# Sparse attention: the compressed branch's scores formed inside the unit loop, one key-value group at a time

## What is computed

```python
s = jnp.einsum('bgmqd,bgnd->bgmqn', qb, kc)                  # kc: 31 compressed keys per group
p_cmp = masked_softmax(s, cmp_end[None, :] <= tq[:, None])
p_cmp = p_cmp * (tq >= CMP_BLOCK - 1).astype(jnp.float32)[:, None]
o_cmp = jnp.einsum('bgmqn,bgnd->bgmqd', p_cmp.astype(vc.dtype), vc)
...
o = jnp.stack([o_cmp, o_sel, o_win], axis=-1).reshape(b, NSA_HEADS, Q_BLOCK, d, 3)
return jnp.einsum('bhqdc,bhqc->bqhd', o, gb)                 # gated sum of the three
```

## Time and profile before

| | |
|---|---|
| median of 3 runs | 1906.64 us (1906.56 to 1907.07) |
| the profiled execution | 1915.09 us, its span 1912.6 us |
| PE busy | 1802.2 us, 94% of the span |
| DVE, ACT, POOL busy | 748.1, 562.1, 201.2 us |
| attention's units (L1424 to L1457) | 733.9 to 834 us in the span |

### The profile page before, as it was taken

The page is one execution under the profiler, slowest core; times in us unless marked ns, Lnnn a source line. Parts: engine busy times, 40 slices in busy tenths (PEclk is TensorE's granted clock), DMA queues, the critical chain, the costliest instruction groups (busy, mean ns, idle before and its releaser), DMA issues. The chain is left out here.

```text
span 1912.6 us, 21769 instructions
## 1 busy us (share of the span) xinstructions
PE 1802.2 (94%) x9065; PEld 1337.2 (70%) x9065; DVE 748.1 (39%) x1121; ACT 562.1 (29%) x871; POOL 201.2 (11%) x229
## 2 busy tenths in 40 slices
PE   7998999999999999998999999989999987999993
PEld 6777888888878786567888888878777773333331
DVE  4425322233265345735222232362345553222334
ACT  4325222232252124635222222352346410000001
POOL 3000000000001103310000000000001102323322
PEclk9979999999999998999999999999999987999997
DMA  7212333322323117312333323233220056999983
GB/s 225 95 39 66 95 103 88 108 90 90 109 95 109 66 58 221 99 34 61 105 88 107 91 89 110 89 121 94 72 111 23 17 206 271 371 381 396 381 325 145
DMA packets 178451, 260.21 MB, mean 136 GB/s; under 512 B 18873, under 2 KB 134777, under 8 KB 165953
## 3 DMA queue, kind: packets, MB, share of 16 engines
q1 hardware_dynamic: 154768, 202.56, 31.6%
q0 software_dynamic: 19568, 27.13, 4.5%
q10 hardware_dynamic: 4032, 29.36, 3.9%
HBM read 296.78 MB, written 29.40 MB: 171 GB/s over the span
## 5 line engine op out<-in xcount | busy, mean ns | idle before, releaser
L149 DVE TENSOR_TENSOR RING_R<-RING,RING_R 128x2048 fp32r<-128x2048 f32 (+1 forms) x110 | 250.2, 2277 | 664.9 <-ACT RING_R L146 664.9
L168 PE MATMUL PB<-RING_R,OPS_R 128*128 128x512 f32 (+1 forms) x1056 | 415.1, 393 | 11.1 <-DVE RING_R L149 5.2
L169 PE MATMUL PB<-RING_R,OPS_R 128*128 128x512 f32 (+1 forms) x1056 | 410.0, 388 | 0.0
L170 PE MATMUL PB<-RING_R,OPS_R 128*128 128x512 f32 (+1 forms) x1056 | 409.9, 388 | 0.0
L146 ACT ACTIVATE RING_R<-RING 128x2048 fp32r<-128x2048 f32 (+1 forms) x110 | 208.4, 1897 | 333.5 <-DMA RING<-in_ffn_w_down 138.1
L168 PE MATMUL PB<-OPS_R,RING_R 128*128 128x512 f32 (+1 forms) x736 | 282.5, 384 | 7.9 <-DVE OPS_R L275 7.9
L169 PE MATMUL PB<-OPS_R,RING_R 128*128 128x512 f32 (+1 forms) x736 | 281.8, 383 | 0.0
L170 PE MATMUL PB<-OPS_R,RING_R 128*128 128x512 f32 (+1 forms) x736 | 281.7, 383 | 0.0
L168 PEld LDWEIGHTS PB<-RING_R,OPS_R 128*128 128x128 f32 x1056 | 199.6, 189 | 54.9 <-DVE RING_R L149 6.9
L170 PEld LDWEIGHTS PB<-RING_R,OPS_R 128*128 128x128 f32 x1056 | 199.5, 189 | 41.0
L169 PEld LDWEIGHTS PB<-RING_R,OPS_R 128*128 128x128 f32 x1056 | 199.9, 189 | 39.1
(11 more groups left out here) (361 smaller groups left out, 1883.9 us busy)
## 6 DMA issues: line engine op xcount, KB each, us to landing
RING<-in_ffn_w_gate SPq DMA_DIRECT2D x44, 512.0 KB, 4.0
RING<-in_ffn_w_up SPq DMA_DIRECT2D x44, 512.0 KB, 5.2
RING<-in_ffn_w_down SPq DMA_DIRECT2D x44, 512.0 KB, 3.9
RING<-in_w_expert_gate SPq DMA_DIRECT2D x16, 1024.0 KB, 8.1
RING<-in_w_expert_up SPq DMA_DIRECT2D x16, 1024.0 KB, 11.6
OPS<-in_w_expert_gate SPq DMA_DIRECT2D x16, 1024.0 KB, 11.3
OPS<-in_w_expert_up SPq DMA_DIRECT2D x16, 1024.0 KB, 13.4
Y<-in_w_expert_down ACTq DMA_DIRECT2D x14, 1024.0 KB, 9.5
```

The source lines that it names most:

```text
L149: nc.vector.tensor_tensor(RING_R[:, raw], RING[:, raw], RING_R[:, high].bitcast(fp32), ALU.subtract).then_inc(s_wlo, 1)
L168: nc.tensor.matmul(o, x[0], w[0], start=start, stop=False)
L169: nc.tensor.matmul(o, x[0], w[1], start=False, stop=False)
L170: return nc.tensor.matmul(o, x[1], w[0], start=False, stop=stop)
```

## The change

The compressed scores are no longer formed ahead of the loop. `cmp_scores(a)` forms those of one group in bank 7: group 0 in step 0, group 1 in step 1, each after `scores(u + 2)` and `values(u - 1)` and ahead of `turned(u)`. The second waits until DVE has taken the first out of bank 7. PE's wait ahead of the loop goes. DVE takes each group by itself (`cmp_max`, 128x512) at the end of steps 0 and 1. Exponential, sum and POOL's scaling come one step later (2; 3; 3 and 4), and the values of `a_cr` are renumbered.

```diff
@@ nsa_pe @@
+            def cmp_scores(a):
+                if a:
+                    pe.wait_ge(a_cr, 2)
+                h = slice(a * DH, (a + 1) * DH)
+                nc.tensor.matmul(PB[:, 7, :], ident_b[:], cmask_b[:].unsqueeze(2).to_broadcast([P, MT, 4, NQ]),
+                                 start=True, stop=False)
+                for i in range(MT):
+                    for c in range(4):
+                        t = nc.tensor.matmul(PB[:, 7, (4 * i + c) * NQ:(4 * i + c + 1) * NQ], qTn[h, c, i * P:(i + 1) * P],
+                                             kcT[h, :], start=False, stop=(i == MT - 1 and c == 3))
+                t.then_inc(a_cs, 1)
+
             def turn_cmp(a):
-                pe.wait_ge(a_cr, 6 + a)
+                pe.wait_ge(a_cr, 8 + a)
@@ nsa_pe, ahead of the loop and in it @@
-            for a in range(2):
-                nc.tensor.matmul(PB[:, 4 + a, :], ident_b[:], cmask_b[:].unsqueeze(2).to_broadcast([P, MT, 4, NQ]),
-                                 start=True, stop=False)
-            for i in range(MT):
-                for c in range(4):
-                    for a in range(2):
-                        h = slice(a * DH, (a + 1) * DH)
-                        t = nc.tensor.matmul(PB[:, 4 + a, (4 * i + c) * NQ:(4 * i + c + 1) * NQ], qTn[h, c, i * P:(i + 1) * P],
-                                             kcT[h, :], start=False, stop=(i == MT - 1 and c == 3))
-            t.then_inc(a_cs, 1)
             nc.tensor.matmul(PB[:, 6, :], zero_b[:], causal_b[:].unsqueeze(1).to_broadcast([P, MT, P]), start=True, stop=False)
-            pe.wait_ge(a_cr, 2)
             for u in range(NU):
                 if u + 2 < NU:
                     scores(u + 2)
                 if u >= 1:
                     values(u - 1)
+                if u < 2:
+                    cmp_scores(u)
@@ nsa_act @@
-                if u == 1:
-                    act.wait_ge(a_cr, 2)
+                if u == 2:
+                    act.wait_ge(a_cr, 4)
                     nc.scalar.activation(WK[:, 1024:2048], WK[:, 1024:2048], ACT.Exp).then_inc(a_ce, 1)
@@ nsa_dve @@
+            def cmp_max(a):
+                dve.wait_ge(a_cs, a + 1)
+                cs = PB[:, 7, :].rearrange("p (j n) -> p j n", n=NQ)
+                nc.vector.tensor_reduce(cmax[:, a, :], cs, AX.X, ALU.max, negate=True).then_inc(a_cr, 1)
+                dve.wait_ge(a_cr, 2 * a + 1)
+                if a == 0:
+                    dve.wait_ge(*t_gn.at(RH))
+                nc.vector.tensor_tensor(Pc[:, a, :].rearrange("p (j n) -> p j n", n=NQ), cs,
+                                        cmax[:, a, :].unsqueeze(2).to_broadcast([P, 16, NQ]), ALU.add).then_inc(a_cr, 1)
+
             maxima(0)
             maxima(1)
-            dve.wait_ge(a_cs, 1)
-            cs = PB[:, 4:6, :].rearrange("p a (j n) -> p a j n", n=NQ)
-            nc.vector.tensor_reduce(cmax[:], cs, AX.X, ALU.max, negate=True).then_inc(a_cr, 1)
-            dve.wait_ge(a_cr, 1)
-            dve.wait_ge(*t_gn.at(RH))
-            nc.vector.tensor_tensor(Pc.rearrange("p a (j n) -> p a j n", n=NQ), cs,
-                                    cmax[:].unsqueeze(3).to_broadcast([P, 2, 16, NQ]), ALU.add).then_inc(a_cr, 1)
             for u in range(NU):
                 normed(u)
                 if u + 2 < NU:
                     maxima(u + 2)
-                if u == 2:
+                if u == 3:
                     dve.wait_ge(a_ce, 1)
                     nc.vector.tensor_reduce(cden[:], Pc.rearrange("p a (j n) -> p a j n", n=NQ), AX.X, ALU.add).then_inc(a_cr, 1)
@@ nsa_dve, end of the loop body, after the copy of bank 5 @@
+                if u < 2:
+                    cmp_max(u)
@@ nsa_pool @@
-                if u in (2, 4):
-                    a = u // 2 - 1
-                    pool.wait_ge(a_cr, 5)
+                if u in (3, 4):
+                    a = u - 3
+                    pool.wait_ge(a_cr, 7)
```

More of the change, by code:

```diff
@@ L1529, in nsa_act @@
                     exps(u + 1)
-                if u == 1:
-                    act.wait_ge(a_cr, 2)
+                if u == 2:
+                    act.wait_ge(a_cr, 4)
                     nc.scalar.activation(WK[:, 1024:2048], WK[:, 1024:2048], ACT.Exp).then_inc(a_ce, 1)
                 if u in CMP_AT:
-                    act.wait_ge(a_cs, CMP_AT[u] + 2)
+                    act.wait_ge(a_cs, CMP_AT[u] + 3)
                     nc.scalar.activation(PTc[:, CMP_AT[u], :], PB[:, 7, :], ACT.Copy).then_inc(a_cp, 1)
@@ L1575, in nsa_dve @@
                     maxima(u + 2)
-                if u == 2:
+                if u == 3:
                     dve.wait_ge(a_ce, 1)
                     nc.vector.tensor_reduce(cden[:], Pc.rearrange("p a (j n) -> p a j n", n=NQ), AX.X, ALU.add).then_inc(a_cr, 1)
-                    dve.wait_ge(a_cr, 3)
+                    dve.wait_ge(a_cr, 5)
                     nc.vector.reciprocal(cden[:], cden[:]).then_inc(a_cr, 1)
-                    dve.wait_ge(a_cr, 4)
+                    dve.wait_ge(a_cr, 6)
                     dve.wait_ge(o_gate, 2)
```

## The result

The changed kernel takes 1922.32 us (median of 9 runs, 1918.05 to 1928.14) beside 1907.14 us for the kernel before in the same 9 rounds. The ratio over all runs is 1.0066, with a 95% interval of 1.0047 to 1.0084: slower by 0.66%. The two medians alone would give 1.0080, because five of the nine runs before lie at 1906.6 to 1907.1 and four at 1911.5 to 1918.7, so that their median falls into the lower group; the means, 1922.90 and 1910.46, are 12.4 us apart. The forecast was 1918.7 us and +0.63%, with a range of 1912.0 to 1922.5; the time is in the range, 0.2 us from its upper end.

A forecast was written before the change was run, and what follows sets the result against it. PE was taken to end these steps. Less 1.87 us for the wait, plus two cmp_scores of 7.25, then later steps' shifts, gave +12.1 us; on the median 1906.64 that is 1918.7 us (+0.63%), range 1912.0 to 1922.5.

The forecast's parts named there:

- new wait in step 2: Ahead of turned(2), PE waits for POOL's rows, delayed by cmp_max(1); with the low clock it costs 1.7 us.
- the walk: PE's starts followed step by step through steps 0 to 4, both streams at the low clock: 12.1 us later; chance 0.62.
- Gain of the removed wait: Ahead of the loop, scores(2) waits for exps(0) alone and starts at 740.07, not 741.94: 1.87 us gained.
- No partner: In cmp_scores all 16 matmuls belong to one group, so none run side by side: 3.66 us per group at full clock.
- the pairing rival: Half-height instructions cost 0.059 us anyhow, without loss by pairing: 1908.6 us, to 1912 at the low clock; chance 0.05.
- The clock: PE restarts at the lower level after idling and both streams stay there, 6.80 us each.
- The rivals with a returning clock: Full clock returns for about one stream, 1915.3 us, chance 0.15, or for both, 1912.0 us, chance 0.06.
- Size of `cmp_scores`: One group's mask and stream in step 0 or 1 at the lower clock: 0.45 plus 6.80, 7.25 us.
- Step 3: Its earlier waits of 1.20 and 0.59 us go; it takes 2.7 us instead of 4.48, ending 12.5 us later than before.
- Step 4: DVE's sum chain moves here, holding its copy, then POOL's scaling; turned(4) ends at 769.4 instead of 757.35, 12.1 us later.
- The rule weighed: Skill rule that weight loads overlap matmuls only where row groups differ; trace contradicts it at full height, shows no unpartnered half-height.
- The rival of load and matmul in sequence: In the streams, load and matmul follow each other, at most 0.07 us more each, 64 times: 1923.4 us; chance 0.09.

The follow-up runs named there:

- e1: Changed kernel with both groups' compressed scores in step 0, taken in turn into banks 7 and 6: ratio 1.0037 to the kernel before, stage 110.94 us.
- e2: Changed kernel with each compressed-scores matmul serving both groups, keys on the diagonal, 8 matmuls of 64 columns per step: ratio 1.0034 to the kernel before, stage 107.17 us.
- e3: Changed kernel with 20 dense matmuls of no use in PE's idle stretch ahead of the loop: ratio 1.0065 to the kernel before, stage 111.13 us.
- e7: e2 with the 20 dense matmuls of no use ahead of the loop, as in e3: ratio 0.9990 to the kernel before, stage 101.12 us.
- e8: Kernel before with PE's wait moved behind scores(2) and unit 0's reciprocal between DVE's reduce and subtraction: ratio 0.9972 to the kernel before, stage 99.66 us.
- e11: The same kernel as e8, run again: ratio 0.9986 to the kernel before, stage 99.27 us.
- e5: Changed kernel without the 32 matmuls of the compressed scores, masks alone in bank 7: ratio 0.9992 to the kernel before, stage 99.93 us.
- e10: e8 with 16 full-height diagonal matmuls of 64 columns ahead of the loop and fillers in PE's two short waits: ratio 0.9973 to the kernel before, stage 98.72 us.

## Why the prediction was right

The sign was right, and the relative time nearly (+0.66% against +0.63%). The median, 1922.3 against 1918.7 us, lies in the range but above the 1917 to 1920.5 that the walk gave itself. The mechanism was right too, but for the new wait in step 2. Point by point:

- **Gain of the removed wait**, 1.87: measured 8.06 - 6.18 = 1.88. PE was released by ACT's exponential, as said.
- **No partner.** Right; the stream is 0.218 us per instruction (740 to 746.7), e1 and e2 show that the number of instructions in a row counts and that two groups in turn halve it, and the pairing rival is out (its sum also takes off 0.5 us for which it gives no row).
- **The clock.** Right: both streams at the lower level, and in e3, where the stream starts full, the clock falls in the midst of it; in e7, with the same fillers ahead and other streams, it does not. The rivals with a returning clock did not come.
- **Size of `cmp_scores`**, 7.25: measured 7.53 (739.13 to 746.66), and 7.50. The stream is 6.97 instead of 6.80 and the mask 0.56 instead of 0.45, that is, twice its price at the full clock. Together 0.5 us of the 1.2 that the sum missed.
- **New wait in step 2**: wrong; no wait was seen. DVE began its copy 0.11 us after the end of `turned(1)` and POOL its rows 0.10 us after the reciprocal, both sooner than in the walk (0.2 and 0.25); PE at the lower clock takes 2.5 us for `scores(4)` and `values(1)`, and the first rows are ready by then. In e7, at the full clock, it is there, 1.00 us. Step 2 took 3.65 us (757.51 to 761.16), the walk's 3.75 nearly: its price was the clock.
- **Step 3** took 3.13 us, not 2.7, since the full clock came back only at the end of it. **Step 4** took 4.06, not 3.7; the stall of 0.79 us for DVE's copy is where it was put, and the 0.26 us behind it is for the rows that DVE itself scales (L1613), where the walk had POOL.

Sum to `scores(7)`: measured 36.74 (731.61 to 768.35), before 23.47, so +13.3 against the walk's +12.1. The rest of the difference, 1922.3 less 1918.7 less 1.2 us, that is 2.4, is in no row. It goes with the level of the runs: the forecast was put on a median of 1906.64, in the lower of the two groups of before's runs, while the means of before and after are 12.4 us apart, near the walk's 12.1. In the rounds of the experiments before's median was 1910.2 to 1911.1. That the absolute time stayed in the range, by 0.2 us, was luck in part.

**The rule weighed.** e3 has the row that the kernel before lacked: half-height matmuls without a partner at the full clock, 18 starts in 1.90 us. That is the spacing of the full-height streams, and of pairs before. So the load of the next lies beside the matmul of the same half: at the lower clock, too, 0.218 us stand beside the 0.213 of the full-height stream, where the rival allowed 0.07 more. The rival of load and matmul in sequence, from the Trainium skill's "TensorE: Matmul & The Clock Gate", section "Part 3: Packing small matmuls — row/col tiling", does not hold here. The other half of that section, that different partitions run side by side, is what e1 measured: 64 in the time of 32.

## What to carry to other kernels

A run of short matmuls costs by the number of instructions, each with its weight load (here 0.11 us each at the full clock, 0.21 to 0.22 at the lower), and not by the columns. So before such a run is split, look at whether neighbours share the array: 64 instructions in turn over two halves cost as much as 32 over one. If both halves can't have a bank each, one matmul over the full height with the second operand on the diagonal does the same in one bank. And where a wait guards a bank, move the wait to the instruction that needs the bank before moving the work: that took 1.9 us (e8) and 2.3 us (e11) off the stage, where moving the work put 13.3 on it.

## What the runs showed beside it

Streams differ in what the clock did in them, though PE is busy in all. The half-height stream of 32 columns in the kernel before was followed by the lower level at 739.7, and in e3 the clock fell within one. The full-height streams of 64 columns in e7 left it at 1.00, from the first fillers on past 757, with waits of up to 1 us between. Height alone does not tell them apart: the full-height stream of 36 columns at 1558.61 had the lower level behind it too. And what left the full clock alone did not bring it back: in e2, without fillers, PE stood at 0.50 from 738.0 to 758.2, 20 us, through two full-height streams of 64 columns, where without any stream (e5) it stood there from 739.2 to 749.4, 10 us. Each is one trace. Fillers of no use removed a spell where they stood, and another came later (e10).
